# Two attention branches of one block written as one instruction program, query tiles taken from the last to the first

## What is computed

```python
# compressed: 63 summary keys per group, each over 32 tokens
p_cmp = softmax(where(cend <= t, q @ kc.T * scale, NEG_BIG))
o_cmp = p_cmp @ vc
# selection: importance of each block of 64 tokens, the best 8 are kept
imp   = einsum('bhgtc,cs->bhts', p_cmp, overlap)
idx   = top_k(where(valid, imp, -1) + where(forced, 1000, 0), 8)
# selected: causal attention over the kept blocks only, with a distance bias
o_slc = softmax(q @ k_slc[idx].T * scale - slope * dist) @ v_slc[idx]
o_nsa = g[0] * o_cmp + g[1] * o_slc + g[2] * o_win
```

## Time and profile before

| what | value |
|---|---|
| time, median of 3 runs | 2819.24 us (2817.35 to 2819.33) |
| time of the profiled execution | 2822.95 us |
| its span | 2820.8 us |
| TensorE busy | 2575.7 us, 91% |
| VectorE busy | 1466.9 us, 52% |
| ScalarE busy | 1013.2 us, 36% |
| mean granted TensorE clock | 0.952 |

### The profile page before, as it was taken

One profiled execution on the slowest core, in us unless ns is written; L12 is line 12 of the kernel. 1 busy time (PEld: TensorE's weight loads), 2 busy tenths in 40 slices (PEclk: granted clock), 3 DMA queues, 4 the chain that ended last, 5 costly groups with the idle time before them and its releaser, 6 DMA issues. The chain is left out here.

```text
span 2820.8 us, 34813 instructions
## 1 busy us (share of the span) xinstructions
PE 2575.7 (91%) x12876; PEld 2119.4 (75%) x12876; DVE 1466.9 (52%) x3370; ACT 1013.2 (36%) x2275; POOL 180.5 (6%) x188
## 2 busy tenths in 40 slices
PE   8999986899996679997989999889799999999998
PEld 6887865777985668885658888666578887888877
DVE  5244266855888874218874732478672323223235
ACT  4223132444674442217861232344442223122132
POOL 2000000000000011101200001343000000000000
PEclk9999986799998989999999999899799999999999
DMA  4112120000000054110011132000541111111113
GB/s 149 31 46 78 56 62 1 1 1 1 1 1 1 1 175 116 38 27 14 25 53 49 49 131 101 30 1 1 194 157 38 49 55 47 49 49 46 49 55 143
DMA packets 105079, 153.05 MB, mean 54 GB/s; under 512 B 35408, under 2 KB 49872, under 8 KB 104912
## 3 DMA queue, kind: packets, MB, share of 16 engines
q1 hardware_dynamic: 96464, 125.67, 14.1%
q0 software_dynamic: 3840, 12.59, 1.1%
q10 hardware_dynamic: 4608, 12.58, 1.1%
HBM read 121.44 MB, written 29.36 MB: 53 GB/s over the span
## 5 line engine op out<-in xcount | busy, mean ns | idle before, releaser
L202 PE MATMUL banks<-mhT,mmwhi 128*128 128x512 f32 x1024 | 316.1, 390 | 3.9 <-ACT qsq L2925 2.8
L193 PE MATMUL banks<-mmwhi,fT 128*128 128x512 f32 x1024 | 315.6, 390 | 3.7 <-ACT qsq L2925 3.7
L193 PE MATMUL banks<-g1whi,hT 128*128 128x512 f32 (+1 forms) x1024 | 304.8, 381 | 7.9 <-ACT gates L428 2.9
L177 DVE TENSOR_TENSOR mmwlo<-mmwraw,mmwhi 128x512 fp32r<-128x512 f32 x144 | 97.1, 689 | 368.8 <-ACT mmwhi L172 368.8
L172 ACT ACTIVATE mmwhi<-mmwraw 128x512 fp32r<-128x512 f32 x144 | 89.3, 629 | 412.6 <-DMA mmwraw<-in_w_down 206.6
L193 PEld LDWEIGHTS banks<-mmwhi,fT 128*128 128x128 f32 x1024 | 191.8, 188 | 45.1 <-ACT qsq L2925 5.4
L202 PEld LDWEIGHTS banks<-mhT,mmwhi 128*128 128x128 f32 x1024 | 191.6, 188 | 45.4 <-ACT qsq L2925 4.1
L193 PEld LDWEIGHTS banks<-g1whi,hT 128*128 128x128 f32 x1024 | 188.7, 189 | 45.9 <-issue 4.4
L202 PE MATMUL banks<-mhT,mmwlo 128*128 128x512 f32 x512 | 199.3, 389 | 0.0
L193 PE MATMUL banks<-mmwlo,fT 128*128 128x512 f32 x512 | 199.3, 389 | 0.0
L193 PE MATMUL banks<-g1wlo,hT 128*128 128x512 f32 (+1 forms) x512 | 194.2, 379 | 0.0
(11 more groups left out here) (443 smaller groups left out, 5444.0 us busy)
## 6 DMA issues: line engine op xcount, KB each, us to landing
mmwraw<-in_w_up SPq DMA_DIRECT2D x64, 256.0 KB, 2.7
mmwraw<-in_w_down SPq DMA_DIRECT2D x64, 256.0 KB, 2.6
g1wraw<-in_w_in SPq DMA_DIRECT2D x56, 256.0 KB, 2.7
g3wraw<-in_w_in SPq DMA_DIRECT2D x40, 256.0 KB, 2.6
qx<-x_scratch SPq DMA_DIRECT2D x16, 512.0 KB, 6.8
xt<-in_x SPq DMA_DIRECT2D x8, 512.0 KB, 5.1
z_scratch<-zst POOLq DMA_DIRECT2D x16, 256.0 KB, 4.1
cw<-in_cmp_w SPq DMA_DIRECT2D x2, 2048.0 KB, 10.0
```

Of the source, the lines that this page charges most:

```text
L177: self.nc.vector.tensor_tensor(self.lo[n][:, c], self.raw[n][:, c], f32(self.hi[n][:, c]), ALU.subtract)\
L193: ins = self.nc.tensor.matmul(out, l, r[:, c], start=k == 0 and i == 0, stop=k == self.nk[j] - 1 and i == 2)
L202: ins = self.nc.tensor.matmul(out, l[:, col], r, start=k == 0 and i == 0, stop=k == self.nk[j] - 1 and i == 2)
```

## The change

`cmp_stage` and the selected `attention_stage` are replaced by one stage, `select_stage`. It goes through the tiles from 7 to 0. The compressed steps of tile 7 stand ahead of the units. The compressed steps of every other tile c are spread over the units of tile c + 1: scores (S) and the first two parts of the VectorE work (F, F2) in the last three units of tile c + 2, the exponent (E), the normalisation (N), the transposes (T), importance and ranking (I, I2), the values (O), the gated output (G) and the transpose of the mask (Z) in the first five units of tile c + 1. For tile 6 the scores and F, F2 stand ahead of the units. There is one score buffer `csc` in place of two. A set of compressed scores takes a bank in the turn of the score banks, a compressed result takes one in the turn of the two value banks, and the compressed transposes take chunks in the turn of the copies. The window stage is as before.

```diff
+    XR, H = 4, NSA_HEADS
+    tiles = list(range(NT - 1, -1, -1))
+    units = [(t, h) for t in tiles for h in range(H)]
+    NU = len(units)
...
+    def at(step, u):
+
+        if u < 0:
+            return None
+        i, r = divmod(u, H)
+        if i == 0 and FIRST[step] == r:
+            return tiles[1]
+        i, r = divmod(u - LATER[step], H)
+        if r == 0 and 1 <= i < NT - 1:
+            return tiles[i + 1]
+        return None
+
+    FIRST = {"S": -1, "F": -1, "F2": -1, "E": 0, "N": 1, "T": 2, "I": 2, "I2": 2, "O": 3, "G": 4, "Z": 3}
+    LATER = {"S": -3, "F": -2, "F2": -1, "E": 0, "N": 1, "T": 2, "I": 2, "I2": 3, "O": 3, "G": 4, "Z": 4}
...
+    def place(key, two):
+        nonlocal nb
+        nb += nb % 2 if two else 0
+        mine = [nb % 4, nb % 4 + 1] if two else [nb % 4]
+        freed_by[key] = [user[m] for m in mine if m in user]
+        bank_of[key] = nb % 4
+        user.update((m, key) for m in mine)
...
+            def out_bank(o):
+                if o >= 2:
+                    pe.wait_ge(o_done, o - 1)
+                return psum[6 + o % 2]
...
+            cmp_scores(NT - 1)
+            cmp_scores(NT - 2)
+            turn_chunk(0)
+            cmp_values(NT - 1)
+            turn_chunk(1)
+            for u in issue[0]:
+                scores(u)
+            for u in range(NU):
+                for n in issue[u + 1]:
+                    scores(n)
+                pe.wait_ge(e_ready, u + 1)
+                for c in of_unit[u]:
+                    turn_chunk(c)
+                for c in after_unit[u]:
+                    turn_chunk(c)
+                if u >= 1:
+                    values(u - 1)
+                if at("O", u) is not None:
+                    cmp_values(at("O", u))
+                if at("S", u) is not None:
+                    cmp_scores(at("S", u))
...
+            front(NT - 1)
+            front2(NT - 1)
+            dve.wait_ge(c_one, 1)
+            norm(NT - 1)
+            importance(NT - 1)
+            ranking(NT - 1)
+            evacuate(dve, 1, nc.vector.tensor_copy, dev)
+            gated(NT - 1)
+            bias_max(0)
+            front(NT - 2)
+            front2(NT - 2)
+            for u in issue[0][1:]:
+                bias_max(u)
+            for u in range(NU):
+                if u >= 1:
+                    evacuate_all(of_unit[u - 1])
+                    evacuate_all(after_unit[u - 1])
+                for n in issue[u + 1]:
+                    bias_max(n)
+                if u >= 2:
+                    output(u - 2)
+                for step, work in (("G", gated), ("F", front), ("F2", front2), ("N", norm), ("I", importance),
+                                   ("I2", ranking)):
+                    c = at(step, u)
+                    if c is not None and (step not in ("I", "I2") or c >= 4):
+                        work(c)
...
-    cmp_stage(nc, sem, mem, C, nqT, kcT[0], kcT[1], vbd, gates, o_nsa, selT, psum, 153)
...
+    select_stage(nc, sem, mem, C, nqT, kcT[0], kcT[1], vbd, ksT,
+                 lambda k, g: kv1[:, k, 384 + g * HD:384 + (g + 1) * HD], gates, o_nsa, selT, psum2, psum,
+                 153, 169, 177, 184)
...
-    attention_stage(nc, sem, "sl", mem, C,
```

More of the change, by code:

```diff
@@ L950, in _ @@
             last.then_inc(tk, 1)
[L954 to L1035, removed]
-                nc.vector.tensor_tensor(x[:], x[:], s[:, 0, :].unsqueeze(2).to_broadcast(m8),
-                                        ALU.subtract).then_inc(e_in, 1)
-            def gated_output(t):
-                dve.wait_ge(o_ready, t + 1)
-                gate = gates[:, t, 0:NSA_HEADS].unsqueeze(2).to_broadcast([P, NSA_HEADS, HD])
-                nc.vector.tensor_tensor(o_nsa[:, t, :].rearrange("p (h d) -> p h d", h=NSA_HEADS),
-                                        psum[3 + t % 2][:].rearrange("p (h d) -> p h d", h=NSA_HEADS),
-                                        gate, ALU.mult).then_inc(o_done, 1)
-            front(0)
-            dve.wait_ge(one, 1)
[L1048 to L1051, removed]
-                dve.wait_ge(e_out, t + 1)
-                ch.link(nc.vector.tensor_reduce(s[:, 1, :], x[:], AX_X, ALU.add))
-                ch.link(nc.vector.reciprocal(s[:, 2, :], s[:, 1, :]))
-                if t == 0:
-                    ch.link(nc.vector.tensor_tensor(x[:], x[:], C["cvalid"][:].unsqueeze(1).to_broadcast(m8),
-                                                    ALU.mult))
-                nc.vector.tensor_tensor(x[:], x[:], s[:, 2, :].unsqueeze(2).to_broadcast(m8),
-                                        ALU.mult).then_inc(p_ready, 1)
-                if t >= 1:
-                    gated_output(t - 1)
-                if t >= 4:
-                    dve.wait_ge(p_ready, t + 1)
-                    if t >= 5:
-                        dve.wait_ge(selt_ready, t - 4)
-                    ch.link(nc.vector.tensor_reduce(imp[:, :, 1:65],
-                                                    x[:].rearrange("p (v g) c -> p v c g", v=NSA_KV), AX_X, ALU.add))
-                    ch.link(nc.vector.tensor_reduce(rank[:, 0, :, :],
-                                                    imp[:, :, 0:64].rearrange("p v (s o) -> p v s o", o=4),
-                                                    AX_X, ALU.add))
-                    ch.link(nc.vector.tensor_tensor(rank[:, 0, :, :], rank[:, 0, :, :], imp[:, :, 4:65:4], ALU.add))
-                    nb = [P, NSA_KV, N_SEL]
-                    ch.link(nc.vector.tensor_tensor(rank[:, 0, :, :], rank[:, 0, :, :],
-                                                    C["selV"][:, t - 4:t - 3, :].to_broadcast(nb), ALU.mult))
-                    ch.link(nc.vector.tensor_tensor(rank[:, 1, :, :], rank[:, 0, :, :],
-                                                    C["selA"][:, t - 4:t - 3, :].to_broadcast(nb), ALU.add))
-                    for v in range(NSA_KV):
-                        ch.link(nc.vector.max(top8[:, v, :], rank[:, 1, v, :]))
-                        ch.link(nc.vector.match_replace(rank[:, 2, v, :], top8[:, v, :], rank[:, 1, v, :], -2.0))
-                    nc.vector.tensor_scalar(rank[:, 3, :, :], rank[:, 2, :, :], -2.0, MASKED, ALU.is_gt,
-                                            ALU.mult).then_inc(sel_ready, 1)
-                    dve.wait_ge(selt_ready, t - 3)
-                    nc.vector.tensor_copy(selT[:, t - 4, :, :],
-                                          psum[5][0:N_SEL, 0:2 * P].rearrange("p (v q) -> p v q", v=NSA_KV))\
-                        .then_inc(selt_done, 1)
-            gated_output(NT - 1)
```

260 lines of the change are left out of this document (255 added, 5 removed).

## The result

| what | before | after |
|---|---|---|
| median of 4 runs each | 2819.26 us (2817.35 to 2819.33) | 2871.91 us (2868.77 to 2880.78) |
| ratio, 95% interval | | 1.019 (1.0177 to 1.0202) |
| profiled execution, its span | 2822.95, 2820.8 us | 2872.54, 2870.6 us |
| TensorE busy | 2575.7 us | 2637.4 us |
| mean granted clock | 0.952 | 0.933 |

The account below looks back on a forecast made before the run. The compressed stage was taken as bound by latencies, the selected stage by TensorE. 448.2 + 122.8 + 13.9 + 12 + 4 + 66.8 - 0.8 = 666.9 instead of 690.2, 23.3 us gained: 2796 us, range 2784 to 2808 (own range 2790 to 2802).

Parts of the forecast that it names:

- step 1: Tile 7's compressed steps, alone ahead of the units: first unit's scores start about 448.2, 12.4 us after the stage's start.
- step 4: Large units starting at half clock: low level 18.5 us, ending near 470, plus 2.2 us idle; 12 us lost, bounds 8 and 17.
- step 3: Compressed work on TensorE between units of tiles 7 to 4, all on the path: 13.9 us.
- step 5: Bank turns after compressed values: next unit's values wait for the preceding unit's output, four places, 4 us, bounds 0 and 8.
- steps 2 to 5: Tiles 7 to 4: units 122.8 us of TensorE, compressed work 13.9, half-clock start 12, new bank-turn wait 4.
- step 6: Tiles 3 to 0, VectorE filling up: 51.8 us as measured plus compressed work on the path, 66.8 us in sum.
- the rival of the clock: Clock does not come up in tiles 7 to 4: 127 us more, 2923 us, slower than before; chance 0.04.
- The rule weighed: Weight-load share, 74% in tiles 7 to 4, leaves TensorE a quarter free; step 3 would vanish, 2782 us; prediction rejected it.
- Room on TensorE for the change: Small matmuls slip in beside the units' weight loads, so step 3 costs nothing: 2782 us; chance 0.08.
- Costlier handing over: Tiles 6 to 0 lose 1.3 us more each, or clock falls once in tiles 3 to 0: 2805 us; chance 0.22.
- The spread does what it says: Rival denied this: compressed steps chain up, units stand still, no gain, 2819 to 2822 us; chance 0.02.

Follow-up runs that it names:

- e5_late_out: Changed kernel with compressed and mask transposes behind the scores of two units ahead, and the output ahead of `bias_max`: 2792.04 us, ratio 0.9901.
- e12_change_nomask: Changed kernel without the matmul that adds the selection mask, so the selected branch attends all keys before a query: 2796.48 us, ratio 0.9912.
- e13_change_rows: Changed kernel with the mask's matmul operands given 128 rows, 112 of them zero: 2799.21 us, ratio 0.9917.
- e14_best_rows: e5_late_out with tile 6's front ahead of the first `bias_max` and the mask's matmul over 128 rows: 2769.38 us, ratio 0.9816.
- e2_rev: Kernel before, with only the selected stage's tile order turned to 7 to 0: 2823.22 us, ratio 1.0023.
- e7_gap18: Kernel before, with eighteen useless VectorE operations once in a unit of tile 5 of the selected stage: 2881.32 us, ratio 1.0202.
- e1_late: Changed kernel with only the compressed and mask transposes moved behind the scores of two units ahead: 2849.49 us, ratio 1.0116.
- e15_gap_rows: e7_gap18 with the mask's matmul over 128 rows, 112 of them zero: 2812.72 us, ratio 0.9967.
- e11_gap_nomask: e7_gap18 without the matmul that adds the selection mask: 2801.43 us, ratio 0.9934.
- e4_asc_late: e1_late with tiles from 0 to 7 and the compressed steps of tile c + 1 in the units of tile c: 2843.7 us, ratio 1.0104.
- e8_out: Changed kernel with only the output moved ahead of `bias_max`: 2852.46 us, ratio 1.0083.
- e3_gap: Kernel before, with ten useless VectorE operations once in a unit of tile 5 of the selected stage: 2829.91 us (2818.23 to 2884.18), ratio 1.0052.

## Why the prediction was wrong

What stood: the first unit's scores start 12.15 us after the stage's start (step 1 said 12.4). The second unit's scores waited 2.23 us (step 4 said 2.2). Compressed values at 2.4 GHz took 529.38 - 528.52 = 0.86 us (step 3 took 1.0). The values waited for an output 5 times, 4.6 us in all, the longest 1.1 (step 5 said 4 us in four places). In e5_late_out, where the clock holds, 32 units from the first scores (448.01) to their last output (599.45) took 151.4 us; steps 2 to 5 give 122.8 + 13.9 + 12 + 4 = 152.7, or 148.7 without the 4 us of waits that this kernel no longer has. Its last 32 took until the window stage at 662.80, 63.4 us; step 6 said 66.8. The window stage was forecast for 666.9, and e5_late_out's median of 2792 lies within the forecast's own range. So with the clock of that kernel the sum is right to a few us. That e12_change_nomask and e13_change_rows come to 2796 and 2799 as well is chance: they save 17 us and more at the mask's matmul and lose as much or more at the waits that they keep (30 us lie between e13_change_rows and e14_best_rows, which is without them).

**The step that failed is step 4, with the place that the rival of the clock had.** It took the low level to last 18.5 us, as before, and to come once. In the changed kernel it held for 39.68 us of TensorE's busy time at the start and 133.11 us from 535 on. If half of these 172.8 us is lost, as the prediction reckons, that is 86.4 us against the 9.8 counted: 76.6 more. The traces put it lower. Between the same instructions, the compressed values of two tiles, the changed kernel took 61.52 us, of which 55 at the low level, and e5_late_out 34.52 us at the high level (first two rows changed kernel, last two e5_late_out):

```profile
528.52 1.11 PE L1383 MATMUL banks<-vbd,slpt 128*128 128x128 f32 x8
590.04 2.02 PE L1383 MATMUL banks<-vbd,slpt 128*128 128x128 f32 x8
...
515.90 1.11 PE L1383 MATMUL banks<-vbd,slpt 128*128 128x128 f32 x8
550.42 1.11 PE L1383 MATMUL banks<-vbd,slpt 128*128 128x128 f32 x8
```

TensorE was busy for 59.02 us of the one and for 34.20 of the other, and these 24.8 us more are 45% of the 55. At that rate the 172.8 us cost some 78 us (an estimate), 68 more than counted. The compressed and selected work took 313.55 us from the first scores to the window stage against 231.0 forecast, 82.5 more. The last 32 units have 4.7 us of this (71.5 us instead of 66.8, with three low stretches), and the waits that step 5 did not have, told below, another 5.3; the last 4 to 5 us stay open. From the -23.3 us of the sum, 82.5 us more make 59, and the runs show 53, the difference being the scatter of the rest of the program and a stage that started 1.8 us earlier.

Two readings led there. First, the 18.5 us came from a stretch with small units, which have no mask matmul. The prediction noted that before, small units stood there, and took the length for the large ones all the same; its bound of 17 us for the loss had no row behind it either. e2_rev, the order of tiles alone, has 35 us, and e7_gap18 140. Second, the rival was given 0.04 because 18.02 busy of 18.50 us brought the clock back. Its own point of decision, 47 us of further low clock, was passed more than three times over (172.8 - 19.6 = 153 us); 2923 was for all of tiles 7 to 4 and was not reached, as the clock did come up for 44 us.

**A wait was missed.** Step 5 looked for waits in the turn of the value banks and found that one. It left out the turn of the two transpose banks, though the order of instructions shows the mask's transposes as the third chunk of their unit. These waits were 5.3 us in three places, a small term, and the longest, 2.25 us, is what the clock fell behind. The 1.2 us of step 5 would have done as well (e1_late). Priced as lengths both are small, and what they cost is what follows them. The Trainium skill, page TensorE: Matmul & The Clock Gate, section A second HAM failure mode: psum-queue depth-cycling, has this as micro-idles between groups of matmuls; the runs agree on the mechanism. The same page of the Trainium skill, section What's actually happening, has activity release the throttle; e7_gap18 speaks against that for this mix of instructions, with 128 of 128 us busy at 0.50.

**The rule weighed** was half right. The Trainium skill (Perfetto Trace Analysis, Identifying the Most-Contended Engine) has weight loads as the measure, which stood at 74% in tile 7, and the prediction answered that there was no hole to fill. There was one of 0.27 us at each mask matmul, covered in the rows by matmuls whose modelled lengths touch. With 128 rows the share rises to 26.14 of 30.00 us in e15_gap_rows, 87%, and 17 us come free. But the change's own matmuls could not use it: e5_late_out took 151.4 us, and the sum without the 13.9 of step 3 would be 138.8.

**The rivals.** Room on TensorE for the change: no. Costlier handing over: not in e5_late_out beyond a few us. The spread does what it says: VectorE's busy time in the stage is 165.93 us, against about 160 forecast.

## What to carry to other kernels

Where a change brings waits of 1 us or more into a stretch in which TensorE was full, they are not priced by their length: ask how long this kind of unit took to get the clock back, from a row with the same matmuls, and test it with a gap of useless operations, over some ten executions where the gap is short. In a loop with two banks in turn, count the chunks of each turn; a third one waits for the other engine's next turn. A matmul with few rows among full ones can be worth giving 128 rows with zeros: here 17 us without the change, 21 us with its waits removed, and 73 us in the change as it stands.

The best kernel of the study is e14_best_rows, with the compressed work spread, both groups of waits taken away and the mask on 128 rows: 2769.38 us, 1.8% under before.

## What the runs showed of the hardware

- With the 16-row mask matmul in its units, TensorE stayed at 1.2 GHz for 140 us while busy throughout (e7_gap18); with 128 rows it was back after 7 us (e15_gap_rows), without the matmul after 6 (e11_gap_nomask). Whether it is the rows themselves or the 0.3 us that the next weight load comes later was not told apart.
- The clock fell behind waits of 1.00 us (e4_asc_late), and did not behind one of 1.07 us in the changed kernel (at 494), one of 1.30 in e8_out (at 479) and one of 1.28 in the profiled execution of e3_gap, whose ten times spread over 66 us. What decides near this length is not shown. The same kernel may fall or not, and medians of few runs are to be read with that in mind.
- A stretch with 55 us at 1.2 GHz had TensorE busy for 24.8 us longer than the same instructions at 2.4 GHz, so the low level cost 45% of its time and not half (changed kernel against e5_late_out).
- A weight load behind a 16-row one came 0.32 us later and behind a 128-row one at once. The Trainium skill, page TensorE: Matmul & The Clock Gate, section Step-by-step: what each phase is for, has loads pulled ahead of running matmuls when their row groups don't conflict or a background buffer is free; here it was the narrow one that was not passed.
